# Operands of a split-precision decoder layer placed at other bytes of their partitions

## The reference

```python
# 1. hybrid mixer
z = x @ w_in + b_in                    # 1024 -> 8192 columns
z_pool, z_lru, z_b, z_c, z_h, z_gate = split(z)
y_pool = multiscale_pool(z_pool, pool_w, pool_scale)       # windows 2, 4, 8, 16, four 256x256 products
y_lru  = rg_lru(conv4(z_lru), lru_w_r, lru_w_i, ...) @ lru_w_out   # eight 128x128 heads for r and i
y_conv = (z_b * conv3(z_c * z_h)) @ sconv_w_out
merged = sum(sigmoid(z_gate[b]) * y for b, y in enumerate((y_pool, y_lru, y_conv)))
mix = merged @ w_mix_out
# 2. cross-attention, 4 heads of 256
q, k, v = x @ w_q, mem @ w_k, mem @ w_v
o = softmax(q @ k.T / 16) @ v @ w_o
# 3. SwiGLU, width 2816
ff = (silu(x @ w_gate) * (x @ w_up)) @ w_down
```

## The kernel before

| at | tensors |
|---|---|
| 0 | xT_h, xT_l (byte 18432 on), raw, wh (67840), wl (84224), act32, st, lru_h, cnv_h and their low parts, memT, pT, kT, qT, v_h, v_l, hidden |
| 192 | xa, xb, xc, x12, xf, ta, tb, tf |
| 32 | p_h, p_l, vr_h, vr_l |
| 128 | ident, par |

## Time and profile before

### The profile page before, as it was taken

How to read it: one execution, slowest core, us unless ns; L and a number is a source line. 1 busy time by engine, 2 the same in 40 slices (tenths; PEclk the granted TensorE clock), 3 DMA queues, 4 the chain that set the end, 5 groups by cost and what they waited for, 6 DMA issues and landing times.

```text
span 1016.1 us, 15300 instructions
## 1 busy us (share of the span) xinstructions
PE 999.2 (98%) x6172; PEld 896.2 (88%) x6172; DVE 690.1 (68%) x866; ACT 482.9 (48%) x669; POOL 44.1 (4%) x36
## 2 busy tenths in 40 slices
PE   8999999999899999999999999999999999999997
PEld 8888888888899998888888998889999999988885
DVE  5767476798898885455675555479988888742336
ACT  4454745446475573223444443356545555532232
POOL 1010000001000000000130000040000000000000
PEclk9999999999999999999999999999999999999999
DMA  6334233232243344235163332204443342333212
GB/s 210 111 96 125 85 103 103 66 106 76 85 124 106 104 154 157 64 124 207 42 207 125 110 98 83 83 23 145 125 125 103 106 125 84 127 122 121 86 42 84
DMA packets 89371, 111.03 MB, mean 109 GB/s; under 512 B 2764, under 2 KB 81760, under 8 KB 89312
## 3 DMA queue, kind: packets, MB, share of 16 engines
q1 hardware_dynamic: 87344, 103.82, 31.8%
q0 software_dynamic: 1824, 6.32, 1.9%
q10 hardware_dynamic: 144, 0.05, 0.0%
HBM read 108.09 MB, written 2.10 MB: 108 GB/s over the span
## 4 chain that ended last, share of the span: by engine, by line
PE 92%; DVE 3%; ACT 2%; DMA 1%; issue 1%; POOL 0%; SPq 0%; DVEq 0%; ACTq 0%
PE ps L752 31%; PE ps L754 30%; PE ps L753 30%; DMA act<-in_x 1%; PE ps L781 1%; DVE xnat L1766 1%; DVE xT_l L1716 0%; ACT ps L1270 0%; PE ps L1035 0%; POOL wl L715 0%; DVE probs L1757 0%; ACT wh L1228 0%; DVE wl L1930 0%; DVE wl L1708 0%; ACT wh L1320 0%
## 5 line engine op out<-in xcount | busy, mean ns | idle before, releaser
L1708 DVE TENSOR_TENSOR wl<-raw,wh 128x1024 fp32r<-128x1024 f32 (+1 forms) x106 | 124.8, 1182 | 148.0 <-ACT wh L1228 147.0
L1228 ACT ACTIVATE wh<-raw 128x1024 fp32r<-128x1024 f32 (+1 forms) x112 | 113.9, 1027 | 200.8 <-PE ps L754 182.5
L752 PE MATMUL ps<-xT_h,wh 128*128 128x512 f32 (+1 forms) x544 | 193.7, 356 | 1.3 <-DVE xT_l L1716 1.3
L754 PE MATMUL ps<-xT_h,wl 128*128 128x512 f32 (+1 forms) x544 | 193.0, 355 | 0.0
L753 PE MATMUL ps<-xT_l,wh 128*128 128x512 f32 (+1 forms) x544 | 192.8, 354 | 0.0
L1930 DVE TENSOR_TENSOR wl<-raw,wh 128x1024 fp32r<-128x1024 f32 x72 | 87.5, 1223 | 55.7 <-ACT wh L1320 55.6
L1320 ACT ACTIVATE wh<-raw 128x1024 fp32r<-128x1024 f32 x72 | 75.5, 1057 | 99.2 <-PE ps L754 64.5
L752 PE MATMUL ps<-wh,st_h 128*128 128x512 f32 x304 | 118.8, 391 | 0.0
L753 PE MATMUL ps<-wl,st_h 128*128 128x512 f32 x304 | 118.3, 389 | 0.0
L754 PE MATMUL ps<-wh,st_l 128*128 128x512 f32 x304 | 118.3, 389 | 0.0
L752 PEld LDWEIGHTS ps<-xT_h,wh 128*128 128x128 f32 x544 | 102.6, 189 | 15.8 <-DVE xT_l L1716 1.5
(11 more groups left out here) (287 smaller groups left out, 2077.6 us busy)
## 6 DMA issues: line engine op xcount, KB each, us to landing
raw<-in_w_in SPq DMA_DIRECT2D x19, 1024.0 KB, 5.6
raw<-in_ffn_w_down SPq DMA_DIRECT2D x11, 1024.0 KB, 4.8
raw<-in_w_in SPq DMA_DIRECT2D x20, 512.0 KB, 3.7
raw<-in_ffn_w_gate SPq DMA_DIRECT2D x20, 512.0 KB, 4.3
gb<-in_ffn_w_up SPq DMA_DIRECT2D x10, 512.0 KB, 4.1
raw<-in_ffn_w_up SPq DMA_DIRECT2D x10, 512.0 KB, 4.4
raw<-in_lru_w_out SPq DMA_DIRECT2D x8, 512.0 KB, 3.4
raw<-in_sconv_w_out SPq DMA_DIRECT2D x8, 512.0 KB, 3.3
```

What stands on the lines that cost most here:

```text
L752: nc.tensor.matmul(dst, st, mv_, start=start, stop=False, skip_group_check=shared)
L754: return nc.tensor.matmul(dst, st_lo_part, mv_, start=False, stop=stop, skip_group_check=shared)
L1228: nc.scalar.activation(wh[:, ring(phase, s), 0:size], src, ACT.Copy).then_inc(w_hi.sem, 1)
L1708: nc.vector.tensor_tensor(wl[:, slot, 0:size], src, wh[:, slot, 0:size].bitcast(F32), ALU.subtract).then_inc(w_lo.sem, 1)
```

## The change

- A slot of wh and wl has 1024 + 64 elements, 4352 bytes. Weights are written (ACT, DVE and POOL) and read (PE) from byte 0, 64 or 192 of their slot, by `w_at`: 64 for the first unit of A's first pass, for P1, P2 and P3 of B, and for K of each head; 192 for V of each head; 0 for all others.
- p_h, p_l, vr_h and vr_l move from 32 to 0 past a multiple of 256, kT_h and kT_l from 0 to 192.
- par, corr, inv_win, cur and soft, small tables of parameters, are declared elsewhere to make room. xT moves 1024 bytes down, what lies behind the ring 1024 up, what lies behind kT 1280 up: these stay where they were past a multiple of 256. u, ws and zl, working rows of stage A, go 32 bytes down with p and vr.

No instruction is added or taken away, and no wait.

```diff
+W_SPARE = 64
+SMALL_PAD = 16
...
-        par = sb("par", [P, DECAY_EXP + 1, KT])
-        corr = sb("corr", [P, GROUPS, POOL_PAD])
-        inv_win = sb("inv_win", [P, GROUPS])
...
-        sb("to_2k", [P, 20])
+        sb("to_1k", [P, SMALL_PAD])
...
-        wh = sb("wh", [P, SPLIT_SLOTS, 1024], F32R)
-        wl = sb("wl", [P, SPLIT_SLOTS, 1024], F32R)
+        wh = sb("wh", [P, SPLIT_SLOTS, 1024 + W_SPARE], F32R)
+        wl = sb("wl", [P, SPLIT_SLOTS, 1024 + W_SPARE], F32R)
...
-            sb("to_p_h", [P, SEQ - (SCONV_TAPS - 1)], F32, scope)
+            sb("to_p_h", [P, SEQ - (SCONV_TAPS - 1) - 8], F32, scope)
...
             cnv_h = sb("cnv_h", [P, KT, SEQ], F32R, scope)
+            par = sb("par", [P, DECAY_EXP + 1, KT], F32, scope)
+            corr = sb("corr", [P, GROUPS, POOL_PAD], F32, scope)
+            inv_win = sb("inv_win", [P, GROUPS], F32, scope)
+            cur = sb("cur", [P, DECAY_EXP + 1, 2], F32, scope)
+            soft = sb("soft", [P, 8, KT], F32, scope)
...
+        sb("to_kT", [P, 48])
         kT_h = sb("kT_h", [P, 2, M], F32R)
         kT_l = sb("kT_l", [P, 2, M], F32R)
+        sb("past_kT", [P, 16])
...
+        def w_at(phase, s):
+
+            if phase == "A":
+                return 16 if s < 2 else 0
+            n = FIRST[phase] + s
+            if B0 <= n < C0:
+                return 16 if n - B0 in [b_step(m, name) for m in range(B_SETS) for name in ("P1", "P2", "P3")] else 0
+            if D0 <= n < E0:
+                return (16, 48, 0)[(n - D0) // 2 % 3]
+            return 0
+
+        def w_slot(w, phase, s, size=1024):
+            at = w_at(phase, s)
+            return w[:, ring(phase, s), at:at + size]
...
-                    h_, l_ = (w[:, ring(phase, s), :].rearrange("p (k n) -> p k n", k=4) for w in (wh, wl))
+                    h_, l_ = (w_slot(w, phase, s + BODY[phase]).rearrange("p (k n) -> p k n", k=4) for w in (wh, wl))
```

More of the change, by code:

```diff
@@ L710, in split @@
             def split(phase, s):
-                n, slot = FIRST[phase] + s, ring(phase, s)
+                n = FIRST[phase] + s
                 pool.wait_ge(w_hi.sem, w_hi.done(n))
                 pool.wait_ge(w_lo.sem, w_lo.done(n - 1))
-                nc.gpsimd.tensor_tensor(wl[:, slot, :], raw_part(phase, s)[0], wh[:, slot, :].bitcast(F32),
+                nc.gpsimd.tensor_tensor(w_slot(wl, phase, s), raw_part(phase, s)[0], w_slot(wh, phase, s).bitcast(F32),
                                         ALU.subtract).then_inc(w_lo.sem, 1)
@@ L877, in product @@
                 weights_ready(phase, 0, n)
-                h_, l_ = (w[:, ring(phase, n), :].rearrange("p (k n) -> p k n", k=4) for w in (wh, wl))
+                h_, l_ = (w_slot(w, phase, n).rearrange("p (k n) -> p k n", k=4) for w in (wh, wl))
                 mh, ml = x_part_
@@ L910, in out_half @@
                 weights_ready("B", 0, n)
-                h_, l_ = (w[:, ring("B", n), :].rearrange("p (k n) -> p k n", k=4) for w in (wh, wl))
+                h_, l_ = (w_slot(w, "B", n).rearrange("p (k n) -> p k n", k=4) for w in (wh, wl))
                 for l in range(2):
@@ L1227, in split @@
                 src, size = raw_part(phase, s)
-                nc.scalar.activation(wh[:, ring(phase, s), 0:size], src, ACT.Copy).then_inc(w_hi.sem, 1)
+                nc.scalar.activation(w_slot(wh, phase, s, size), src, ACT.Copy).then_inc(w_hi.sem, 1)
             def turned(first, t, bank, dst, width):
@@ L1284, in _ @@
                     act.wait_ge(first_in, 16)
-                    nc.scalar.activation(wh[:, 0, :], raw[:, 0, 0:1024], ACT.Copy).then_inc(w_hi.sem, 1)
+                    nc.scalar.activation(w_slot(wh, "A", 0), raw[:, 0, 0:1024], ACT.Copy).then_inc(w_hi.sem, 1)
                 if t == 2:
                     wait_raw(act, "A", 0, 0)
-                    nc.scalar.activation(wh[:, 1, :], raw[:, 0, 1024:2048], ACT.Copy).then_inc(w_hi.sem, 1)
+                    nc.scalar.activation(w_slot(wh, "A", 1), raw[:, 0, 1024:2048], ACT.Copy).then_inc(w_hi.sem, 1)
             split("A", 0, -1)
@@ L1315, in w_high @@
             def w_high(phase, n, src, ready):
-                slot = ring(phase, n)
                 act.wait_ge(weights_used.sem, weights_used.done(FIRST[phase] + n - SPLIT_SLOTS))
                 act.wait_ge(*ready)
-                nc.scalar.activation(wh[:, slot, :].rearrange("p (k n) -> p k n", k=4), src,
+                nc.scalar.activation(w_slot(wh, phase, n).rearrange("p (k n) -> p k n", k=4), src,
                                      ACT.Copy).then_inc(w_hi.sem, 1)
@@ L1706, in split @@
                 src, size = raw_part(phase, s)
-                slot = ring(phase, s)
-                nc.vector.tensor_tensor(wl[:, slot, 0:size], src, wh[:, slot, 0:size].bitcast(F32),
+                nc.vector.tensor_tensor(w_slot(wl, phase, s, size), src, w_slot(wh, phase, s, size).bitcast(F32),
                                         ALU.subtract).then_inc(w_lo.sem, 1)
@@ L1927, in w_low @@
             def w_low(phase, n, src):
[L1928 removed]
                 dve.wait_ge(w_hi.sem, w_hi.done(FIRST[phase] + n))
[L1930 to L1931 removed]
+                nc.vector.tensor_tensor(w_slot(wl, phase, n).rearrange("p (k n) -> p k n", k=4), src,
+                                        w_slot(wh, phase, n).rearrange("p (k n) -> p k n", k=4).bitcast(F32),
                                         ALU.subtract).then_inc(w_lo.sem, 1)
```

12 lines of the change are left out of this document (3 added, 9 removed).

## The result

| | before | after |
|---|---|---|
| median, us (20 runs each) | 1025.86 | 1015.41 |
| lowest, highest | 1018.13, 1028.32 | 1013.71, 1025.42 |
| profiled execution | 1017.87 | 1014.57 |
| its span | 1016.1 | 1012.8 |

The account below looks back on a forecast made before the run. The prediction took TensorE (PE), with work in flight 98% of the span, as the bound; 0.64 + 0.68 + 2.13 + 0.16 + 2.40 = 6.0 us off 1019.2 gave 1013.2 us, with an 8-in-10 range of 1010.5 to 1017.5.

Parts of the forecast that it names:

- A, first unit: Stage A: four half steps of 24 matmuls with weights moved to byte 64 save 0.16 us each, 0.64 us.
- p and vr: Stage A: moving operands p and vr go from byte 32 to 0, saving 0.17 us in each of 4 passes, 0.68.
- B: Stage B: 17 steps with weights at 64 save 2.38 us, less a new wait of 0.25, leaving 2.13.
- D, head 0: Stage D, first head: only the scores count, 0.16 us; savings of K and V go into a wait.
- D, heads 1 to 3: Stage D, later heads: K, V and scores save five steps of 0.16 us, 0.80 a head, 2.40 in all.
- rival 1: The moving operand's own start counts, not the pair, so weights at 64 gain nothing: 2.3 us saved, 1016.9; chance 0.12.
- rival 2: A stationary operand at 64 hurts in A's first unit, B and K: 2.3 us slower, 1021.5; chance 0.06.
- rival 4: No effect at all; slow and fast go with the tile, not its address: 1019.2 us; chance 0.04.
- Rival 5: More than forecast: weights at 64 beat (192, 0) on 27 steps, up to 4.3 us more, 1008.9; chance 0.07.
- (0, 64) is the same as (192, 0), and a step costs 2.72 us: Pairs (moving, stationary), bytes past a multiple of 256: equal distance was taken as equal time for 24 matmuls, unseen in the trace.
- Some 40 such meetings at 7 ns either way are at most 0.3 us: Where steps of two kinds meet, one matmul streams at 192 while weights at 64 load; at most 0.3 us.
- rival 3: Stage B: DVE, 90% busy, can't follow, so B gives nothing back: 3.9 us saved, 1015.3; chance 0.06.

Follow-up runs that it names:

- e1: Kernel of matmuls alone, layer left out: all 64 pairs of moving and stationary starts in steps of 32 bytes; 256 columns took 113.3 to 120 ns each.
- e3: Kernel of matmuls alone: four pairs of distance 192, each behind six other groups and a wait, three times; 113.3 or 117.8 ns a matmul.
- e5: The changed kernel with weights at byte 224 instead of 64 (A's first unit, B's P1 to P3, K); median 1023.77 us, ratio to before 0.9992.
- e9: e8 with the weights of K's first half at byte 192, its second half at 64 as before; median 1014.13 us, ratio to before 0.993.
- e4: The changed kernel with xT at 192, weights at 0 for A's first unit and B, 192 for 512-column steps of A and Q; median 1014.08 us, ratio 0.9948.
- e7: Kernel of matmuls alone: (192, 0), then (192, s), then (192, 0), entered slow and fast; the last group took 113.3 or 117.8 ns a matmul.
- e6: The changed kernel with P1 of F's sets 1 and 5 at weights 64; 5 runs at 1014.5 to 1016.2 us, ratio to before 0.9965.
- e8: e4 with P1 of every set of B and F at weights 128, pair (192, 128); median 1013.57 us, ratio to before 0.9925.
- e10: The changed kernel run once more, nothing altered; median 1015.66 us, ratio to before 0.9952.
- e11: Operand places of before, with the new slot spacing and moved tables, and P1 of every set of F at weights 128; median 1019.9 us, ratio 1.0006.
- e12: The changed kernel with P1 of F's set 1 at weights 192, pair (192, 192); median 1022.42 us, ratio to before 1.0036.

## Why the prediction was right or wrong

By its own steps, each with the saving of the profiled pair:

| step | forecast | measured |
|---|---|---|
| A, first unit | 0.64 | 0.49 |
| p and vr | 0.68 | 0.65 |
| B | 2.13 | 0.35 |
| D, head 0 | 0.16 | 0.04 |
| D, heads 1 to 3 | 2.40 | 1.45 |
| sum | 6.0 | 3.0 |

The span fell by 3.3. The other 0.3 is 0.2 at the start of the program, where the loads of x came sooner, 0.15 in the first matmuls behind p and vr and 0.05 in P1 of B's set 0, less 0.1 in the pause of F. The sum came out at half of the forecast, and by its number rival 1 (2.3 us) was nearer; that V fell and B and K hardly did is also what was put down as the sign of rival 1, and only e1 tells the two apart.

**The variable was right, but not the whole of it.** "How far the moving operand stands ahead of the stationary one modulo 256" is what e1 shows, and "the moving operand's own start is what counts" (rival 1, 1016.9), "a stationary operand at 64 hurts" (rival 2) and "no effect" (rival 4) fall by the same map. Rival 5 as well: no pair was below 113.3.

**The price of the pair was wrong.** The step that failed is "(0, 64) is the same as (192, 0), and a step costs 2.72 us". It is the same in distance and not in time, since distance 192 has two spacings, and what runs ahead has its part in which one comes. In A's first unit (0, 64) did run at 113.3 in three of four half steps. In B 17 steps won 0.037 us each (2.861 to 2.824) where 0.14 were put down, 0.63 in place of 2.38. K won 0.107 a head where 0.32 were put down, the scores 0.045 where 0.16. V, entered behind K, won its 0.30 a head as forecast. The earlier trace rows show only fast groups of distance 192, so one spacing looked like the price of the pair. But the trace of before had a slow one. In B's last set a product with tb, at (192, 0), stands among the 512 columns of the output projections. Timeline of the kernel before, PE:

```profile
373.42 0.39 PE L754 MATMUL ps<-lru_h,wl 128*128 128x512 f32 x1
...
373.64 0.28 PE L752 MATMUL ps<-tb,wh 128*128 128x256 f32 x1
...
376.47 0.28 PE L752 MATMUL ps<-xT_h,wh 128*128 128x256 f32 x1
```

It took 2.83 us, 118 ns a matmul, and the forecast counts tb among the fast ones. That a pair of distance 192 can be slow, behind 512 columns for one, could be read before the change was made. The forecast had also set the time of 1027.02 aside; by its distance from the rest it was an execution with F at the second spacing, which is inferred, as none of before was profiled in its upper group.

**Small meetings were not small.** "Some 40 such meetings at 7 ns either way are at most 0.3 us" counted one matmul each. The neighbour's effect lasts the whole step (e3, e5, e9), and F, once slow, stayed so for 185 us (e4).

**The waits were right in kind.** DVE follows in B: 17.56 of 19.42 us busy, no wait for wl, and rival 3 falls. The step behind bq's copy took 2.796 instead of 2.743 us, a new wait of 0.06 where 0.25 was put down for PE 0.42 early; it was only 0.11 early. The wait at 260 grew from 2.98 to 3.07 us from start to start, that of head 0 by 0.08, as less had been won ahead of it. The product behind the wait at 260, at (192, 0), ran at 118 and took 2.93 us instead of 2.85. With these three, 0.35 us is left of the 0.63 that B's 17 steps won. Writes at 64 and 192 bytes into a slot cost nothing: DVE's took 1223 and ACT's 1058 ns on average, against 1222 and 1057 in the earlier trace rows.

**The rule against it.** e1 shows two groups with the same moving start at 120.0 and 117.8 ns, (0, 0) and (0, 64), and with 512 columns 226.7 and 233.4, (0, 0) and (0, 128): where the weights lie does reach the running matmuls. The Trainium skill ("TensorE: Matmul & The Clock Gate", step 1 of "Step-by-step: what each phase is for") has the two read ports independent and says of bandwidth that the loading takes none from the running matmul; in timing the runs don't agree with it for this type of operand.

What stays open: why a distance has two spacings, why pairs of one distance differ behind the same neighbour (e1), and what in a pause decides which one PE comes back with.

## What to carry to other kernels

Time a matmul by the distance of starts within a step, and set all steps of one shape side by side, the odd ones at the seams of stages too: a difference of some ns between them may be the place of their operands, by their distance modulo 256 bytes. Before a price is taken over to a pair that no row shows, ask what runs ahead of it and behind it, and try the pair among its neighbours with a kernel of matmuls alone. When executions of one kernel fall into two groups, take the profile of each and compare the spacing stage by stage; here one product in seven at another distance removed the upper group, and an execution in it costs about twice the 4 us that all the placements had won.

## What the runs showed of the hardware

- Matmuls of float32r operands with a weight load each run at 113.3 to 120 ns from start to start for 256 columns at the full granted clock, by the distance of their operands (113.3 or 117.8 at 192, 116.7 mostly at 32, 120 at 0); for 512 columns at 226.7 to 228.0 (distance 0), 229 (64) or 232 to 235 (all others) (e1).
- At distance 192 both 113.3 and 117.8 are stable. Which one comes depends on the group ahead, its spacing included, and is the same in each repetition (e3, e7). Behind 512 columns the four pairs of e3 were all slow, and so was (192, 0) in B of the kernel before (118 ns); in e1 three of eight pairs were fast there.
- A stretch at (192, 0) kept the slower spacing for 185 us in F, until its end (e4), and could fall to it at a pause without any change of pair (e4, e5, e6, e8); 24 matmuls at (192, 128) end it (e7, e8) and take 113.3 or 117.8 ns each themselves.
- After the same wait of 2.8 us the granted clock came back at either of its levels in different executions, 1.0 or 0.80 to 0.83 over the 8 us behind it, a difference of 1.5 us (after; e5, e10, e11, e12).
